# Delta rule in a two-block layer: another split of its VectorE and ScalarE work, a rounded two-product decay sum, and all first products in half 0

## The reference, cut to what matters

```python
proj = rmsnorm(x, g_pre) @ w_in                      # qkv, z_a, b_raw, a_raw, ...
q, k, v = silu(short_conv(qkv)); q, k = l2norm(q), l2norm(k)
gc = jnp.cumsum(g, axis=-1)                          # log decays, within a chunk
decay = jnp.exp(where(causal, gc[i] - gc[j], -inf))
kb = k * beta
A = (kb @ k.T) * decay * strict
T = inverse(eye + A)                                 # unit lower triangular, 64 x 64
u, w = T @ (v * beta), T @ (kb * jnp.exp(gc))
qk, q_dec = (q @ k.T) * decay, q * jnp.exp(gc)
k_end = k * jnp.exp(g_last - gc)
# over the chunks, state S = 0 at first:
v_new = u_n - w_n @ S
o = qd_n @ S + qk_n @ v_new
S = S * jnp.exp(gl_n) + ke_n.T @ v_new
```

## Time and profile before

| | us |
|---|---|
| median of 3 runs | 2368.41 |
| the three runs | 2366.63, 2368.41, 2372.14 |
| the profiled execution | 2367.83 |
| span of its trace | 2366.2 |
| PE busy | 2340.8 (99%) |
| DVE busy | 1627.0 (69%) |
| ACT busy | 1174.6 (50%) |
| POOL busy | 233.7 (10%) |

### The profile page before, as it was taken

The page is one execution under the profiler, slowest core; times in us unless marked ns, Lnnn a source line. Parts: engine busy times, 40 slices in busy tenths (PEclk is TensorE's granted clock), DMA queues, the critical chain, the costliest instruction groups (busy, mean ns, idle before and its releaser), DMA issues.

```text
span 2366.2 us, 35125 instructions
## 1 busy us (share of the span) xinstructions
PE 2340.8 (99%) x13692; PEld 1923.5 (81%) x13692; DVE 1627.0 (69%) x2147; ACT 1174.6 (50%) x1554; POOL 233.7 (10%) x410
## 2 busy tenths in 40 slices
PE   8999999999999999999999999999999999999998
PEld 7888888777777777788888888888888888888887
DVE  5899999878787878656665756666666544555565
ACT  5555555576454545444555654535353444443443
POOL 3000000112121213011000101001010000000100
PEclk9999999999999999999999999999999999999999
DMA  7566666766555658488655557776776755676673
GB/s 252 187 213 204 204 196 228 234 205 232 179 187 179 191 175 286 152 289 284 217 194 194 193 173 240 229 229 233 225 239 223 247 192 185 230 260 190 223 252 125
DMA packets 239247, 506.87 MB, mean 214 GB/s; under 512 B 15065, under 2 KB 15938, under 8 KB 238210
## 3 DMA queue, kind: packets, MB, share of 16 engines
q1 hardware_dynamic: 214898, 418.57, 53.8%
q0 software_dynamic: 24208, 86.31, 11.4%
HBM read 464.45 MB, written 40.39 MB: 213 GB/s over the span
## 4 chain that ended last, share of the span: by engine, by line
PE 65%; DVE 1%; DMA 1%; ACT 0%; issue 0%; POOL 0%; DVEq 0%; ACTq 0%
PE acc L2604 58%; PE acc L2624 2%; PE acc L2639 1%; PE aux L2666 1%; PE aux L2811 0%; DMA delta_branch_spill<-ol 0%; PE aux L3112 0%; DMA r1l<-delta_branch_spill 0%; PE aux L3117 0%; PE aux L3017 0%; PE aux L2652 0%; PE acc L3017 0%; PE aux L2917 0%; PE aux L2804 0%; PE aux L2904 0%
## 5 line engine op out<-in xcount | busy, mean ns | idle before, releaser
L1644 DVE TENSOR_TENSOR w_lo<-raw,w_hi 128x1024 fp32r<-128x1024 f32 x790 | 962.4, 1222 | 653.7 <-ACT w_hi L960 642.0
L960 ACT CAST w_hi<-raw 128x1024 fp32r<-128x1024 f32 x790 | 824.3, 1049 | 980.7 <-PE acc L2604 938.7
L2604 PE MATMUL acc<-w_hi,r1h 128*128 128x512 f32 x1828 | 722.3, 395 | 3.0 <-DVE w_lo L1644 1.9
L2604 PE MATMUL acc<-w_lo,r1h 128*128 128x512 f32 x1828 | 709.3, 388 | 0.0
L2604 PE MATMUL acc<-w_hi,r1l 128*128 128x512 f32 x1828 | 708.5, 388 | 0.0
L2604 PE MATMUL acc<-w_hi,r2h 128*128 128x512 f32 x1208 | 472.2, 391 | 0.2 <-DVE r2l L1738 0.2
L2604 PE MATMUL acc<-w_hi,r2l 128*128 128x512 f32 x1208 | 470.2, 389 | 0.0
L2604 PE MATMUL acc<-w_lo,r2h 128*128 128x512 f32 x1208 | 470.1, 389 | 0.0
L2604 PEld LDWEIGHTS acc<-w_hi,r1h 128*128 128x128 f32 x1828 | 343.3, 188 | 81.6 <-DVE w_lo L1644 6.3
L2604 PEld LDWEIGHTS acc<-w_hi,r1l 128*128 128x128 f32 x1828 | 343.3, 188 | 72.0
L2604 PEld LDWEIGHTS acc<-w_lo,r1h 128*128 128x128 f32 x1828 | 343.6, 188 | 65.4
(11 more groups left out here) (507 smaller groups left out, 1589.1 us busy)
## 6 DMA issues: line engine op xcount, KB each, us to landing
raw<-in_w_in SPq DMA_DIRECT2D x263, 1024.0 KB, 5.1
raw<-in_w_out SPq DMA_DIRECT2D x32, 1024.0 KB, 5.2
raw<-in_w_br_b SPq DMA_DIRECT2D x16, 1024.0 KB, 5.3
raw<-in_w_br_a SPq DMA_DIRECT2D x16, 1024.0 KB, 7.5
raw<-in_w_ple_gate SPq DMA_DIRECT2D x16, 1024.0 KB, 5.1
raw<-in_w_o_mla SPq DMA_DIRECT2D x16, 1024.0 KB, 5.1
raw<-in_w_o_conv SPq DMA_DIRECT2D x16, 1024.0 KB, 5.2
raw<-in_w_q_b SPq DMA_DIRECT2D x8, 1024.0 KB, 5.1
```

Of the source, the lines that this page charges most:

```text
L960: nc.scalar.copy(w_hi[:, h % HL, 0:n], raw[:, k % RAW, x * HALF:x * HALF + n]).then_inc(hi_ready, 1)
L1644: V.tensor_tensor(w_lo[:, h % HL, 0:n], raw[:, k % RAW, x * HALF:x * HALF + n], w_hi[:, h % HL, 0:n].bitcast(F32), ALU.subtract).then_inc( ...
L2604: ins = T.matmul(acc[:, s, x, 0:n], a[:, kt0 + k, xs_], w[:, h % HL, at], start=start and k == 0 and m == 0, stop=stop and k == kts - 1 an ...
```

## The change

Seven things change, and all are in the delta rule or next to it.

1. DVE makes `gm` at `hl` 29 in place of 31. ACT rounds it into `gmh` at `hl` 30 (`decay_hi`), and DVE takes the rest `gml` at `hl` 31, after the pad step of v.
2. PE multiplies a rounded `strict_r` (the same 0/1 matrix, copied once by ACT) by `gmh` and by `gml`. This replaces the float32 product. It comes first in half 0, before both `kT` products, which now also stand in half 0. ACT takes the exponential at `hl` 1.
3. `kbe` and `ke` move from DVE (4 instructions at `hl` 2) to ACT: 8 activations at `hl` 3 and 10 at `hl` 5, one for each head and tile. The parts that nothing reads (chunk 0 of `kbe`, the last chunk of `ke`) are left out.
4. PE leaves out the w products of chunk 0, where the state is zero (4 of 16 per group), and ACT copies only what is left.
5. `qdT` moves from `hl` 15 to 11 and covers the last 192 of 256 tokens' columns in 4 heads.
6. On DVE the state updates of the scan and the last inversion step (`inv_ready`) move into `delta_first`, so ahead of the weight half of their step.
7. In `OWN` the k row moves its pad, convolution, silu and back steps one half later; in `OWN_FIRST` only its back step does, from 27 to 28.

```diff
-OWN = (..., (16, 0, 20, (20, 22), 23, 24), ...)
-OWN_FIRST = (..., (16, 20, 21, (22, 24), 25, 27), ...)
+OWN = (..., (16, 0, 21, (21, 23), 24, 25), ...)
+OWN_FIRST = (..., (16, 20, 21, (22, 24), 25, 28), ...)
 # ACT
+            def decay_hi(i):
+                act.wait_ge(sem("gm_ready"), i + 1)
+                nc.scalar.copy(gmh[...], gm[...]).then_inc(sem("gm_hi"), 1)
...
-                for n, r in enumerate(CHUNK_ROWS):
-                    act.wait_ge(sem("uw_done"), dv(4, TT + n + 1))
-                    sig(nc.scalar.copy(wT[:, :, :, r]..., X[:, 2 + n]...), "w_ready", dv(2, n + 1))
+                act.wait_ge(sem("uw_done"), dv(4, TT + 1))
+                sig(nc.scalar.copy(wT[:, 1, :, CHUNK_ROWS[0]], X[:, 2, TOK:2 * TOK]...), "w_ready", dv(2, 1))
+                act.wait_ge(sem("uw_done"), dv(4, TT + 2))
+                sig(nc.scalar.copy(wT[:, :, :, CHUNK_ROWS[1]]..., X[:, 3]...), "w_ready", dv(2, 2))
...
-                if hl == 2:
+                if hl == 1:
                     act.wait_ge(sem("decay_done"), dv(1, 1))
                     sig(A(decT[...], X[:, 0], ACT.Exp), "decT_ready", dv(1, 1))
+                if hl == 3:
+                    act.wait_ge(sem("cols_ready"), dv(1, 1))
+                    for x, rows in ((0, CHUNK_ROWS[1]), (1, slice(0, P))):
+                        for h in range(GH):
+                            c.inc(A(kbe[rows, x, h], ktok[rows, x, h], ACT.Copy, scale=dcol[rows, 4, x, h:h + 1]))
+                if hl == 5:
+                    for x in range(TT):
+                        for dst, src, hs in PLACES:
+                            for h in range(hs.start, hs.stop):
+                                if x == 0:
+                                    c.inc(A(ke[dst, x, h], ktok[src, x, h], ACT.Copy, scale=dcol[src, 5, x, h:h + 1]))
+                                elif src.start == 0:
+                                    ...
+                    c.wait()
+                    act.sem_inc(sem("k_scaled"), 1)
 # DVE
-                if hl == 31:
+                if hl == 29:
                     dve.wait_ge(sem("decay_cols"), i + 1)
                     sig(V.tensor_tensor(th(gm), rep(tri_c[:], TC2), over(col(7), SEQ_CHUNK), ALU.mult), "gm_ready", i + 1)
+                if hl == 31:
+                    dve.wait_ge(sem("gm_hi"), i + 1)
+                    sig(V.tensor_tensor(th(gml), th(gm), th(gmh).bitcast(F32), ALU.subtract), "gm_lo", i + 1)
...
-                if hl == 2:
-                    dve.wait_ge(sem("cols_ready"), dv(1, 1))
-                    c.inc(V.tensor_tensor(th(kbe), th(ktok), over(col(4), DK), ALU.mult))
-                    ...
-                if hl == 15:
-                    dve.wait_ge(sem("egc_landed"), dv(32, 32))
-                    sig(V.tensor_tensor(flat(qdT), flat(qT), flat(egc_rep), ALU.mult), "qdT_ready", dv(1, 1))
+                if hl == 11:
+                    dve.wait_ge(sem("egc_landed"), dv(32, 32))
+                    sig(V.tensor_tensor(qdT[:, :, SEQ_CHUNK:], qT[:, :, SEQ_CHUNK:], egc_rep[:, :, SEQ_CHUNK:], ALU.mult), "qdT_ready", dv(1, 1))
 # PE
                 if hl == 0:
-                    pe.wait_ge(sem("tok_ready"), dv(2, 2))
-                    per_chunk(2, columns_of(kT), columns_of(kT)).then_inc(sem("B_done"), 1)
-                if hl == 1:
                     ...
-                    pe.wait_ge(sem("gm_ready"), dv(1, 1))
-                    T.matmul(X[:, 0], strict_lo[:], gm[...], start=True, stop=True).then_inc(sem("decay_done"), 1)
+                    pe.wait_ge(sem("gm_lo"), dv(1, 1))
+                    T.matmul(X[:, 0], strict_r[:], gmh[...], start=True, stop=False)
+                    T.matmul(X[:, 0], strict_r[:], gml[...], start=False, stop=True).then_inc(sem("decay_done"), 1)
+                    pe.wait_ge(sem("tok_ready"), dv(2, 2))
+                    per_chunk(2, columns_of(kT), columns_of(kT)).then_inc(sem("B_done"), 1)
                     per_chunk(1, columns_of(kT), columns_of(qT), True).then_inc(sem("qk_done"), 1)
...
                         for n, r in enumerate(CHUNK_ROWS):
+                            if (x, n) == (0, 0):
+                                continue
                             ins = T.matmul(X[:, 2 + n, ...], kbe[r, x, h], uinv[r, x, h], start=True, stop=True)
```

More of the change, by code:

```diff
@@ L386, in build_layer @@
             qkT = s1("qkT", [P, TT, GH, SEQ_CHUNK])
+            gmh, gml = [s1(n, [P, TT, GH, SEQ_CHUNK], F32R) for n in ("gmh", "gml")]
             state = s1("state", [P, GH, DK])
@@ L1083, in _ @@
                     decays_softplus()
+                if hl == 4:
+                    act.wait_ge(sem("mask_ready"), MASK_TRI)
+                    nc.scalar.copy(strict_r[:], strict_lo[:]).then_inc(sem("strict_ready"), 1)
                 if hl == 6:
@@ L1221, in first_taps @@
                         sig(ins, "tap0_ready", n + 1)
+            def decay_hi(i):
+                act.wait_ge(sem("gm_ready"), i + 1)
+                nc.scalar.copy(gmh[:].rearrange("p t h i -> p (t h i)"), gm[:].rearrange("p t h i -> p (t h i)")).then_inc(sem("gm_hi"), 1)
             def z_tanh(ph, i, first=False):
@@ L1329, in _ @@
                         ln_value(step)
+                if hl == 30:
+                    decay_hi(0)
             z_tanh(ph, 0, True)
@@ L1340, in _ @@
                     own(ph, hl, i, False)
+                    if hl == 30:
+                        decay_hi(i)
                 z_tanh(ph, i)
@@ L1991, in delta_first @@
             def delta_first(hl, dv):
-                for n in range(1, NCH):
-                    x, (rows, out_rows) = n // 2, scan_rows(n)
-                    if hl == 17 + 2 * n:
-                        dve.wait_ge(sem("scan_done"), dv(SCAN, 2 * n))
-                        for h in (0, GH // 2):
-                            v = us[out_rows[h], x, h:h + GH // 2].rearrange("p h d -> p (h d)")
-                            ins = V.tensor_tensor(v, v, X[out_rows[h], 0, h * DK:(h + GH // 2) * DK], ALU.subtract)
-                            if h == 0:
-                                c.inc(ins)
-                        sig(ins, "scan_ready", dv(SCAN, 2 * n))
-                        c.wait()
@@ L2093, in delta @@
                             c.wait()
+                for n in range(1, NCH):
+                    x, (rows, out_rows) = n // 2, scan_rows(n)
+                    if hl == 17 + 2 * n:
+                        dve.wait_ge(sem("scan_done"), dv(SCAN, 2 * n))
+                        for h in (0, GH // 2):
+                            v = us[out_rows[h], x, h:h + GH // 2].rearrange("p h d -> p (h d)")
+                            ins = V.tensor_tensor(v, v, X[out_rows[h], 0, h * DK:(h + GH // 2) * DK], ALU.subtract)
+                            if h == 0:
+                                c.inc(ins)
+                        sig(ins, "scan_ready", dv(SCAN, 2 * n))
+                        c.wait()
@@ new lines, in delta_first @@
+                if hl == 4 + 2 * LEVELS:
+                    dve.wait_ge(sem("lx_done"), dv(LEVELS, LEVELS))
+                    sig(V.tensor_copy(xs_b, blocks(0)), "xs_ready", dv(LEVELS, LEVELS))
+                if hl == 5 + 2 * LEVELS:
+                    dve.wait_ge(sem("ly_done"), dv(LEVELS, LEVELS))
+                    for b in BLOCKS[::2]:
+                        ins = V.tensor_scalar(th(uinv)[b, :, LATE], blocks(0)[b], -1.0, None, ALU.mult)
+                        if b is BLOCKS[0]:
+                            c.inc(ins)
+                    sig(ins, "inv_ready", dv(LEVELS, LEVELS))
+                    c.wait()
@@ L2846, in delta @@
                         pe.wait_ge(sem("oT_lo"), dv(2, 0))
-                    pe.wait_ge(sem("gm_ready"), dv(1, 1))
-                    T.matmul(X[:, 0], strict_lo[:], gm[:].rearrange("p t h i -> p (t h i)"), start=True, stop=True).then_inc(sem("decay_done"), 1)
+                    else:
+                        pe.wait_ge(sem("strict_ready"), 1)
+                    pe.wait_ge(sem("gm_lo"), dv(1, 1))
+                    T.matmul(X[:, 0], strict_r[:], gmh[:].rearrange("p t h i -> p (t h i)"), start=True, stop=False)
+                    T.matmul(X[:, 0], strict_r[:], gml[:].rearrange("p t h i -> p (t h i)"), start=False, stop=True).then_inc(sem("decay_done"), 1)
+                    pe.wait_ge(sem("tok_ready"), dv(2, 2))
+                    per_chunk(2, columns_of(kT), columns_of(kT)).then_inc(sem("B_done"), 1)
                     per_chunk(1, columns_of(kT), columns_of(qT), True).then_inc(sem("qk_done"), 1)
```

116 lines of the change are left out of this document (51 added, 65 removed).

## The result

| | before | after |
|---|---|---|
| median of runs, us | 2368.24 (21 runs, 2365.66 to 2372.14) | 2373.50 (21 runs, 2368.92 to 2376.68) |
| ratio, 95% interval | 1 | 1.0022 (1.0016 to 1.0028) |
| profiled execution, us (span) | 2367.83 (2366.2) | 2370.12 (2368.5) |

The change makes the kernel 5.3 us slower. 2361.8 was predicted, a gain of 6.6. The profiled execution shows 2.3 of the 5.3 us. The other 3 had to be looked for in later ones.

A forecast was written before the change was run, and what follows sets the result against it. PE, busy 2340.8 of 2366.2 us, was taken as the bound. Terms of -2.5, -1.9, -2.8, -0.8, -1.0 and +2.4 summed to -6.6 us: 2361.2 profiled, 2361.8 for the median; 8-in-10 range 2357.5 to 2366.8.

The forecast's parts named there:

- Shared block: After half 0: two rounded decay products and one block of passes in place of two save 0.62 per group, 2.5 us.
- w products: After half 15: leaving out 8 of 32 passes at 0.060 us each saves 0.48 per group, 1.9 us for four.
- the rule for weight loads: At the w products: 107 ns per load of 128 columns; if loads set the pace, the term would be 3.4 us.
- Halves 15 and 16: Earlier `uinv`, q convolution and ACT copies recover PE's waits at the u products and `qT` transposes: -2.8 us.
- Scan and round 0: Earlier state update removes PE's `state` waits, -0.8 us; later `kT` transposes remove a 1.4 us wait, -1.0 us net.
- The 0.4 charged against it: In round 0, an allowance for `gml` of the first group getting tight: 0.4 us, bounds 0 to 1.4.
- `ke` on ScalarE: At step 5, ten copies of 0.306 us delay the next cast; PE waits 0.6 for `xs` per group, +2.4 us.
- the rival with 0.42 a copy: ACT becomes the bound at steps 5 and 6: +7.2 in place of +2.4, 2366.6 us; chance 0.2.
- The rival "the change shortens PE's stream and nothing else": Recovered waits (5.6 us) come back at the next step, as in the k convolution; 2367.4 us; chance 0.05.

The follow-up runs named there:

- e1_q3_first: Changed kernel with GpSimd's load of the last quarter of `conv_branch_spill` issued ahead of the stores of `oh` and `ol`; 2370.1 us, ratio 1.0006.
- e17_q1q3_w: Changed kernel with quarters 1 and 3 of `conv_branch_spill` loaded earlier and all 32 w passes, `ke` copies still at half 5; 2363.5 us, ratio 0.9982.
- e13_q1q3_ke_w: Changed kernel with quarters 1 and 3 of `conv_branch_spill` loaded earlier, `ke` copies at half 7 and all 32 w passes; 2361.6 us, ratio 0.9976.
- e6_all_w: Changed kernel with the eight dropped w passes put back, 32 per group again; 2368.05 us, ratio 0.9996.
- e2_before_q3: Kernel before, with only GpSimd's load of the last quarter of `conv_branch_spill` moved ahead of the stores of `oh` and `ol`; 2368.0 us, ratio 0.9996.
- e9_pad: Changed kernel with 44 increments of an unused semaphore at the start of PE's program, shifting its code only; 2371.7 us, ratio 1.0022.

## Why the prediction was wrong, by its own steps

**Shared block: right.** -2.5 was predicted, the trace gives -3.0. From 568.27 to the second stream row at 571.41 are 3.14 us; less two steps 2.69, against 1.29 + 2.16 before, so 0.75 a group:

```profile
568.50 0.39 PE L2871 MATMUL aux<-gmh,strict_r 128*128 128x512 f32 x1
568.73 0.40 PE L2872 MATMUL aux<-gml,strict_r 128*128 128x512 f32 x1
569.06 1.15 PE L2828 MATMUL aux<-kT 128*64 128x64 f32 x32
570.04 1.10 PE L2828 MATMUL aux<-qT,kT 128*64 128x64 f32 x32
```

**w products: wrong, and this is the term whose reasoning failed.** -1.9 was predicted, 0.0 measured. The earlier trace rows gave 0.060 us a pass by division. That is a mean over passes that run in pairs of 0.11, and the change takes one of a pair. The row was read right and divided by the wrong unit. The prediction's remark that the row contradicts the rule for weight loads rests on the same mean, and falls with it: a single pass takes 0.11 us, not 0.060. The starts of the single passes in the trace of before would have told it.

**Halves 15 and 16: right.** The wait for `uinv` is gone (1.1 in two groups), and PE's delay at the `qT` transposes fell from 1.0 to 0.25 in each of three: 3.4 in all, of 2.8 predicted.

**Scan and round 0: right.** The `state` waits are gone (0.8), and so is the 1.4 at `kT`. The 0.4 charged against it shows up as waits for `w_lo`, 0.3 of it at 553.82. `gml` was in no group late.

**`ke` on ScalarE: the mechanism right, the size short.** +2.4 was predicted, 0.6 a group. Measured are 1.16 in each of three groups, 3.5 in all. In the fourth the late load covers it; where the load is early, the fourth shows 1.14 too (`e1_q3_first`, `e17_q1q3_w`). The first such wait of PE, and the rows of ScalarE ahead of it, in the changed kernel:

```profile
589.71 0.75 PE L2835 MATMUL aux<-xs,tinv 32*32 32x32 f32 x64 [1.09 <-DVE xs L2086]
```

```profile
582.31 1.05 ACT L962 CAST w_hi<-raw 128x1024 fp32r<-128x1024 f32 x1 [0.84 <-PE acc L2628]
583.26 2.12 ACT L1263 ACTIVATE ke<-ktok,dcol 128x128 f32<-128x128 f32 x6
585.41 1.42 ACT L1266 ACTIVATE ke<-ktok,dcol 64x128 f32<-64x128 f32 x4
587.01 1.05 ACT L962 CAST w_hi<-raw 128x1024 fp32r<-128x1024 f32 x1 [0.19 <-ACT ke L1266]
```

Ten copies take 3.57 us, 0.36 each and not 0.306, and the cast behind them waits another 0.19 for their end. The copies come in five couples. Within a couple the second starts 0.31 us after the first, as in the earlier trace rows. From one couple to the next, where the rows or the tile change, it is 0.41. So the row priced a copy within a couple rightly, and what it couldn't show was 0.1 us at each change. 3.57 lies between the forecast's 3.06 and the 4.2 of the rival with 0.42 a copy. Moving the copies gave back 1.9 us by the medians; of the rest, part came back at half 10 behind VectorE's `qkT`.

**The step that decided.** By these terms PE should be, and was, about 5 us ahead when the delta rule's rounds end. The sum then ran to the end of the program as if nothing behind it could be late. The rival "the change shortens PE's stream and nothing else" asked the right question, where the gained time is waited out, but looked for it within the delta rule. It was at the seam from QKVZ to YB, in a load that GpSimd issues behind a 12 us wait and that was ready 0.7 us ahead of PE. And since PE went on at the lower clock level after this wait, the loss was larger than the gain. (That rival's own number has a slip: by the terms of the prediction the recovered waits are 2.8 + 0.8 + 1.0 = 4.6 us, not 5.6, which gives 2366.4.) The second half of the error had no place in the reckoning at all: the edit that saves nothing moves PE's code, and two far places pay for it (near 1588 the pad shows it, at 727 it is argued). The range ended at 2366.8. With the loads and the copies moved and the eight passes back (`e13_q1q3_ke_w`) the kernel takes 2361.6, near the 2361.8 of the sum. That is partly luck: the sum had 1.9 us for w that no run shows, and the waits and the shared block gave more than it said.

Open is how the 5.4 us between the changed kernel and `e6_all_w` divide, and whether they are all of the code's place. The stalls near 1588 cost 1.3 to 3.4 us where they come, the stop at 727 up to 2, and the pad alone, whose profile has neither, gave no shorter time. The rest may be the spread of the medians, or a place that no profile caught. One such place is in the profile of `e2_before_q3`: a wait of 3.3 us for `us` at 655, behind a late landing of `praw`, with 4.3 us lost. No experiment explains it.

## What to carry to other kernels

Before you add up a gain on the critical engine, walk along the program from where it is gained and ask of each load and store ahead of that engine how early it is. The first that is ready by less than the gain is where the sum ends. Price a small product by when the next one starts, pair by pair, not by the mean of the block. When a kernel gets slower far from every edit, look at the instruction packets among the DMAs, and undo first the edits that save nothing.

## What the runs showed of the hardware that I had not expected

- Two passes in the two row halves cost 0.11 us together; one alone costs the same 0.11.
- A 16 KB packet of code within a store of 512 KB goes with 1.1 us more until the next step behind it (6.1 against 5.0), and, through what is queued behind it, with 2.0 us of TensorE 24 us later.
- Waits of 3.55 and 5.25 us for an operand were followed by rows 0.43 us apart in place of 0.23, with a granted clock of 0.75 and 0.66 in the next 10 us. A wait of 2.09 us (`e9_pad`, at 941) was followed by three rows 0.23 apart and then by rows 0.43 apart. After waits of 0.98 and 2.28 us (`e1_q3_first`, at 926 and 1588) the rows stayed 0.23 apart.
- 44 increments of a semaphore in a row stand 0.15 us apart on TensorE, 6.6 us in all. Since TensorE waits for its first transfers then anyway, its first half came only 3.1 us later.
- Small scaled copies on ScalarE start 0.29 to 0.31 us apart one behind the other, and 0.41 where the rows or the tile change.
